# Expert weights with eight neighbouring channels in a partition, and token rows gathered with a stride

## What is computed

```python
xn = rmsnorm(h, g)                       # 512 tokens x 1024 channels, gain g per channel
y = 0
for e in range(N_EXPERTS):               # 32 in block 1 (hidden 256), 16 in block 2 (hidden 512)
    t = silu(xn @ w_gate[e]) * (xn @ w_up[e])
    y = y + combine[:, e:e+1] * (t @ w_down[e])   # combine is 0 but for two experts of each token
h = h + y
```

## Time and profile before

| | us |
|---|---|
| median of three runs | 1838.04 |
| lowest and highest | 1835.74, 1839.43 |
| the profiled execution | 1838.83 |
| its span, first to last instruction | 1837.0 |
| PE busy | 1623.1 |
| DVE, ACT, POOL busy | 545.8, 378.6, 108.3 |

### The profile page before, as it was taken

One profiled execution on the slowest core, in us unless ns is written; L12 is line 12 of the kernel. 1 busy time (PEld: TensorE's weight loads), 2 busy tenths in 40 slices (PEclk: granted clock), 3 DMA queues, 4 the chain that ended last, 5 costly groups with the idle time before them and its releaser, 6 DMA issues. The chain is left out here.

```text
span 1837.0 us, 27496 instructions
## 1 busy us (share of the span) xinstructions
PE 1623.1 (88%) x11633; PEld 898.0 (49%) x11633; DVE 545.8 (30%) x978; ACT 378.6 (21%) x667; POOL 108.3 (6%) x165
## 2 busy tenths in 40 slices
PE   3999988977978999999599996678988999999995
PEld 2434443776456555555344444665455444444442
DVE  2235124423132333232401005935131222122223
ACT  1023036342111111111311003235111111111112
POOL 3000012450000000000000001400000000000000
PEclk9989989999978999999799998869978999999998
DMA  4111100200544998896413100020542668766651
GB/s 172 46 46 46 46 0 0 95 4 8 182 137 146 319 326 306 291 319 213 149 46 137 47 0 1 1 91 2 185 137 88 220 241 274 248 219 222 224 184 57
DMA packets 176880, 251.59 MB, mean 137 GB/s; under 512 B 8771, under 2 KB 140954, under 8 KB 176802
## 3 DMA queue, kind: packets, MB, share of 16 engines
q1 hardware_dynamic: 176624, 250.41, 39.9%
q10 hardware_dynamic: 178, 0.05, 0.0%
HBM read 246.23 MB, written 4.19 MB: 136 GB/s over the span
## 5 line engine op out<-in xcount | busy, mean ns | idle before, releaser
L311 PE MATMUL banks<-mixT,ring 128*128 128x512 f32 x672 | 295.2, 602 | 5.9 <-DVE mixT L289 5.9
L311 PEld LDWEIGHTS banks<-mixT,ring 128*128 128x128 f32 x672 | 129.7, 194 | 171.0 <-issue 164.6
L1827 PE MATMUL banks<-arena_moe,mixT 128*32 128x512 f32 x768 | 178.2, 606 | 0.0
L1310 PE MATMUL banks<-ring,mixT 128*128 128x512 f32 x256 | 115.7, 613 | 8.0 <-PEq L47 8.0
L1827 PE MATMUL banks<-ring,mixT 128*32 128x512 f32 x768 | 121.6, 637 | 0.0
L1310 PEld LDWEIGHTS banks<-ring,mixT 128*128 128x128 f32 x256 | 49.8, 197 | 70.2 <-issue 70.2
L308 PE MATMUL banks<-ring,mixT 128*128 128x512 f32 x192 | 82.9, 592 | 0.0
L1827 PEld LDWEIGHTS banks<-ring,mixT 128*32 128x32 f32 x768 | 32.7, 116 | 79.2 <-issue 79.1
L1514 PE MATMUL banks<-G_moe,x_hi_moe 128*128 128x256 f32 x256 | 65.3, 294 | 6.1 <-DVE G_moe L1639 6.1
L1799 PE MATMUL banks<-G_moe,x_hi_moe 128*128 128x256 f32 x256 | 64.8, 292 | 5.2 <-DVE G_moe L1930 5.2
L1514 PE MATMUL banks<-G_moe,x_lo_moe 128*128 128x256 f32 x256 | 63.8, 288 | 0.0
(11 more groups left out here) (412 smaller groups left out, 2524.9 us busy)
## 6 DMA issues: line engine op xcount, KB each, us to landing
ring<-in_w_in SPq DMA_DIRECT2D x18, 1024.0 KB, 8.5
arena_moe<-in_exp_w_gate SPq DMA_DIRECT2D x16, 1024.0 KB, 11.4
arena_moe<-in_exp_w_up SPq DMA_DIRECT2D x16, 1024.0 KB, 12.0
arena_moe<-in_exp_w_down SPq DMA_DIRECT2D x16, 1024.0 KB, 13.2
ring<-in_exp_w_gate SPq DMA_DIRECT2D x16, 1024.0 KB, 8.0
ring<-in_exp_w_up SPq DMA_DIRECT2D x16, 1024.0 KB, 10.0
ring<-in_exp_w_down SPq DMA_DIRECT2D x16, 1024.0 KB, 11.3
arena_moe<-in_w_gate SPq DMA_DIRECT2D x16, 1024.0 KB, 8.2
```

Source lines behind the costliest of these rows:

```text
L311: last = pe.matmul(bank[:], w[:, c, i * P:(i + 1) * P], m.mixT[:, c, :], start=(c == 0), stop=(c == DC - 1))
L1310: last = pe.matmul(m.banks[k % 3][:], m.mixT[:, c, i * P:(i + 1) * P], w[:, c, :], start=(c == 0), stop=(c == DC - 1))
L1827: last = pe.matmul(hb[u][T * i:T * (i + 1), :], z.xe[:, group[u], j, T * i:T * (i + 1)], both[:, :, j, :], start=(j == 0), stop=(j == DC - ...
```

## The change

A partition now holds eight neighbouring channels: partition p has channels 8p to 8p+7, and chunk j of it is channel 8p + j. Three places follow from that.

- `sources`: gate and up weights are read as `(p c) n -> p c n`. A partition's eight rows are neighbours in the matrix. In block 1, where a row has 256 values, they are 8 KB in one run; in block 2, where a row has 512 values and a slot takes 256 of them, they stay eight pieces of 1 KB, now 2 KB apart. The down weights are loaded as before.
- `gather`: the stationary operand of chunk j is every eighth channel, starting at j, so its 128 columns stand 32 bytes apart in SBUF instead of 4. Number, sizes and order of the matmuls stay.
- `setup_phase`: the two gains of the expert stages are needed in the new order as well. `params` grows from 96 to 112 columns, two loads from ACT's queue write columns 96 to 111, and ACT waits for both (semaphore `permuted`) before the stage's barrier. The old columns stay, for the output stages use them.

```diff
-        self.params = sb("params", [P, 96])
+        self.params = sb("params", [P, 112])
...
+PERMUTED = {"norm_ffn_g": 96, "ffn_norm_2": 104}
...
+            for name, c in PERMUTED.items():
+                act.dma_start(m.params[:, c:c + DC], io[name].rearrange("l (p c) -> (l p) c", c=DC)).then_inc(ph.sem("permuted"), 16)
+            act.wait_ge(ph.sem("permuted"), 32)
...
-        return (wg[:, f0:f0 + 256].rearrange("(c p) n -> p c n", p=P), wu[:, f0:f0 + 256].rearrange("(c p) n -> p c n", p=P),
+        return (wg[:, f0:f0 + 256].rearrange("(p c) n -> p c n", p=P), wu[:, f0:f0 + 256].rearrange("(p c) n -> p c n", p=P),
...
-                                last = pe.matmul(gath[a][:, b * 2 * W:(b + 1) * 2 * W], part[:, t, j * P:(j + 1) * P],
+                                last = pe.matmul(gath[a][:, b * 2 * W:(b + 1) * 2 * W], part[:, t, :].rearrange("p (n c) -> p c n", c=DC)[:, j, :],
...
-                                last = pe.matmul(gath[a][:, b * 2 * P:(b + 1) * 2 * P], rows[:, t, j * P:(j + 1) * P],
+                                last = pe.matmul(gath[a][:, b * 2 * P:(b + 1) * 2 * P], rows[:, t, :].rearrange("p (n c) -> p c n", c=DC)[:, j, :],
...
-        phase_moe(nc, m, io, z, "moe1", COLUMN["norm_ffn_g"], ring[0])
+        phase_moe(nc, m, io, z, "moe1", PERMUTED["norm_ffn_g"], ring[0])
...
-        phase_moe_wide(nc, m, io, z, "moe2", COLUMN["ffn_norm_2"], ring[1])
+        phase_moe_wide(nc, m, io, z, "moe2", PERMUTED["ffn_norm_2"], ring[1])
```

## The result

| | before | after |
|---|---|---|
| median of four runs, us | 1836.89 | 1968.10 |
| lowest and highest | 1835.60, 1839.43 | 1966.54, 1970.28 |
| the profiled execution | 1838.83 | 1966.54 |
| its span | 1837.0 | 1964.8 |

The ratio is 1.0713, with a 95% interval from 1.0695 to 1.0732.

The account below looks back on a forecast made before the run. The prediction took PE, by the gather's pace, as the bound. Profiled execution, strided load, longer runs, setup stage and offset to the median gave 1838.8 + 46.7 + 0 + 0 - 0.8 = 1885 us; range 1836 to 1945 us.

Parts of the forecast that it names:

- The bound: Expert stages: PE, by its instructions' pace, is the bound, not the DMA engines; no PE wait there is for a transfer.
- The cover: Gather: a weight load of 111 ns lies behind a matmul of 120 ns, leaving 9 ns in each of 1024 pairs.
- The price of the stride: Gather's weight loads: 0.45 ns a column from an ACT row, load 111 to 168 ns, 46.7 us; 34 in 100.
- the rival above: The doubled load, in the gather: 222 ns, 1937 or 1949 us; 24 in 100.
- The upper end: Gather: load of 222 ns, a pair 102 ns more, 99.2 us, with 11.6 us on top at the lower clock.
- The doubled load: Gather: weight load takes twice as long, 222 ns; 1937 us, or 1949 with the lower clock's share; 24 in 100.
- more than that: Gather: a load dearer than doubled; three times 111 ns would give 2045 us; 7 in 100.
- The low clock: First gather of each stage: 51 pairs of 217 ns hide a load of 168 ns, so 973 pairs pay.
- The doubled load's extra term: First gathers at the lower clock: load doubles there too, 51 x (444 - 217) ns = 11.6 us on top.
- Parts 2 and 3: Longer load runs in block 1, at most 2.3 us gain; setup stage's two added loads, 0 to 1.5 us; both taken as 0.
- the rival that the loads were a hidden bound: Block 1: faster loads would shorten it by at most 2.3 us, to 1836 us; faster had 4 in 100.
- The free stride: Gather: load keeps its 111 ns or grows by less than the cover; 1838 us; 31 in 100.

Follow-up runs that it names:

- Experiments 4, 5 and 3: In this order step2, step3 and step4: the kernel before with a step of 8, 12 and 16 bytes in the gather's weight loads; 1837.86, 1889.25 and 1951.67 us.
- loads_only: The changed kernel with the gather's unstrided operand put back in both blocks, keeping the new loads and setup stage; 1834.89 us, ratio 0.9998.
- wide_only: The kernel before with the strided stationary operand in block 2's gather only; 1902.70 us.
- turn_strided: The changed kernel with the step also in the weight loads of the output stage's turn, router weights and gain following; 1974.76 us.
- gather_only: The kernel before with the strided stationary operand of the gather alone, in both blocks; 1960.74 us, ratio 1.0691.
- step4: The kernel before with a step of four values (16 bytes) in the gather's weight loads; 1951.67 us.
- step7: The kernel before with a step of seven values (28 bytes) in the gather's weight loads; 1952.46 us.
- step2: The kernel before with a step of two values (8 bytes) in the gather's weight loads; 1837.86 us.
- step3: The kernel before with a step of three values (12 bytes) in the gather's weight loads; 1889.25 us.
- stream_strided: The kernel before with the gather's streamed one-hot matrix read at a step of 32 bytes, weight loads unstrided; 1932.69 us.
- permuted_store: The changed kernel with ACT and DVE writing the high and low rows in the new channel order, so all readers take neighbours; 1837.89 us, ratio 1.0006.

## Why the prediction was wrong, step by step

**The bound: right.** PE, and within it the pace of the gather, was what counted. No wait changed, the gain of the faster loads was nothing, and a body grew by 64 times the difference of the pace: 64 x 0.122 = 7.8 us, and 47.9 instead of 40.1 measured.

**The cover: right.** The load of 111 ns behind a matmul of 120, 9 ns of cover. Experiments 4, 5 and 3 take the load's mean duration in block 1 from 198 to 201, 265 and 329 ns, and the pace goes from 120 to 120, 175 and 233: the first 3 ns stay hidden, and from 12 to 16 bytes 64 ns of load are 58 of pace.

**The price of the stride: this step failed.** "The stride costs 15 ns on 32 values, 0.45 ns each. Carried over to 128 columns that is some 57 ns: the load goes from 111 to 168 ns". It went to 241 ns, 130 more and not 57. To take ACT for the nearest engine was not the mistake. The number was: ACT pays 0.98 ns a value when it reads 1024 of them, and 0.98 x 128 = 125 ns on top of 111 gives 236. The row that gave 0.45 reads 32 values, and its 15 ns were the small difference between instructions that have some 200 ns of fixed time. The prediction said that part of the price can be hidden in those 200 ns, and took the value all the same; that warning, with the small count, should have moved the forecast to the rival above. That the price was hidden in the fixed time is the likely reason for 0.45, but no run has shown it. With 241 ns in the prediction's own sum it would have come to 1838.0 + 973 x 0.121 + 51 x 0.024 = 1957 us, 11 below the result.

**The upper end: too low.** The doubled load was priced at 222 ns, 1937 or 1949 us. The load takes 2.17 times the 111 ns. The rival's mechanism is the one that came, a rate halved by each step to another place, and its condition was too wide: with two columns in each 16-byte line the step costs nothing beyond the 9 ns of cover (experiment 4). The doubled load had 24 in 100, more than that 7, and the range was cut between the two. Against the doubled load itself stood only that it "is more than any row shows". No row had the price at all, so that was no ground.

**The low clock: wrong for the forecast, right in the rival.** The forecast let 51 pairs of the first gathers hide the load. They paid as well: 20 matmuls in 5 us at clock 0.51, the pace of some 244 ns that there is at 1.00. The load's extra time doesn't follow TensorE's clock, as the prediction supposed (that it belongs to the memory is the likely reading, not a shown one), but at 241 ns the load is longer than the 217 ns of a matmul at the lower clock. The doubled load's extra term supposed 444 ns there, which was wrong: what the load takes doesn't follow TensorE's clock.

**Parts 2 and 3: right, at 0.** loads_only shows both together, within 0.15% of nothing. The 8 KB runs came as said in block 1 only; the rival that the loads were a hidden bound falls with it. In the setup stage ACT's queue now moves 466 packets. The rows are queue 10 from 8 to 12 us and from 12 to 16 us, against the earlier trace rows:

```profile
q10 hardware_dynamic: 245, 0.03, 5.1%
...
q10 hardware_dynamic: 133, 0.00, 2.2%
```

From 16 us on it has none, and DVE starts at 21.10 us instead of 21.15.

**The free stride: fell.** The Trainium skill's "TensorE: Matmul & The Clock Gate", section "LDWEIGHTS (loading the stationary operand)", has a load's time go by its columns alone. These traces agree for neighbours, with 111 ns, and for a step of 8 bytes as far as the matmul's 120 ns let one see. They don't for 12 bytes (175 ns), 16 and 28 (233 and 234) and 32 (241). The Trainium skill's "Advanced Engine Details and Errata", section "SBUF Cachelines", penalises a different line at each access. That is the rule that these runs bear out, with 233 ns for 128 columns in as many lines.

**A reading of a row.** Slices 13 and 31 of PE stand at 8 tenths in the earlier trace rows, not at nine, which changes nothing.

**What the prediction did not have: some 9 us in block 2.** 448 pairs of 0.122 us are 54.7, and the seven bodies grew by 60.6; the stretch ahead of them grew by 2.0 more than its gather, and the last body by 1.0. The difference goes with the clock at the starts of bodies. In before it falls to the lower level for 3.4 us around the start of six of eight bodies; after, for 3.4 us in five and for 6.8 us in three, which together are 37.5 us at the lower level instead of 20.5. Two of these stretches, windows of before and of after:

```profile
1561.90:1565.30 3.40, 3.40 (x20) 0.86 (x16) 1.31 (x4) 1.28 (x1) 0.00 (x0) 0.50 0.00 0
```

```profile
1527.80:1534.60 6.80, 6.80 (x36) 2.72 (x39) 1.58 (x5) 1.46 (x3) 0.00 (x0) 0.51 0.00 0
```

PE is busy in all of both. 17 us more at half the speed cost up to 8.5 us, an estimate that covers the difference but for its rounding. The clock's rows of the other runs give 37.5 us in wide_only and turn_strided, 30.7 in gather_only, step4 and step7, 20.5 in loads_only, step2 and step3, and 13.7 in stream_strided. So every run with a load of 233 ns or more has more of it. What decides whether a stretch is long stays open: gather_only has the pace of the whole change and less of the low clock. It is not only that a gather takes longer: with the streamed operand strided (218 ns a pair) the seven bodies of block 2 took 417.0 us, and 375.2 + 448 x 0.097 = 418.7 has no such extra; with the step of 16 bytes (236 ns) they took 429.8, against 375.2 + 448 x 0.114 = 426.3.

## What to carry to other kernels

Before a layout is changed so that a transfer runs in longer pieces, ask who reads the tile afterwards, how often, and whether neighbours in that read still share 16 bytes of SBUF: here a fall of the DMA share from 0.91 to 0.77, which nobody waited for, was paid with 1024 weight loads of 241 instead of 111 ns. Where the order is needed, put the step where the data is written once (13 us of work on engines that had time, and nothing in the result), or behind a matmul longer than the slow load. And a price read off a short instruction, as the difference of two durations that are mostly fixed, can be far too low, as 0.45 instead of 0.98 ns a value was here: if it is to be carried over to something long, give the range above it a good share of the chances.

## What the runs showed of the hardware that had not been expected

- The pace that a weight load of 128 fp32r columns allows goes by the 16-byte lines that its columns touch: 111 ns for neighbours (32 lines), no more than the matmul's 120 at a step of 8 bytes (64), 175 at 12 (96), 233 at 16 and 234 at 28 (128), 241 at 32 (128). The 7 ns between 28 and 32 bytes are not explained.
- The time of the strided load doesn't follow TensorE's clock: the first gather's 64 pairs take 15.30 us, of which the first 4.9 at clock 0.51, and 63 distances of 0.244 us at clock 1.00 are 15.4.
- The streamed operand pays for a step of 32 bytes with 0.85 instead of 0.42 ns a column, and ACT's read of 1024 values with 2047 instead of 1044 ns. With a step of 512 bytes ACT's write of 1024 values takes 2062 instead of 1149 ns, and DVE's instruction, which writes and reads with that step, 1986 instead of 1284.
- The lower clock at the starts of block 2's bodies lasted 30.7 to 37.5 us in sum where the gather's loads took 233 ns or more, and 13.7 to 20.5 us elsewhere (17.1 in permuted_store).
